# Two-layer block kernel: decay rows, mask and splits of the gated delta inverse moved, weight splits ahead of columns and taps

## What is computed

```
for l in range(2):                                        # first block
    mod = (silu(c) @ ada_w[l] + ada_b[l])                 # shift, scale, gate of three sublayers
    x = x + 0.5 * gate0 * swiglu(adaln(x), ffn1_w13[l], ffn1_w2[l])
    p = adaln(x) @ w_in[l] + b_in[l]
    y = concat([rms(nsa(p)), rms(short_conv(p)), gated_deltanet(p), mlstm(p)])
    x = x + gate1 * (y @ w_out[l])
    x = x + 0.5 * gate2 * swiglu(adaln(x), ffn2_w13[l], ffn2_w2[l])
for l in range(2):                                        # second block
    x = x + concat([sgu(n), diff_attention(n)]) @ w_out2[l]
    up = rms(x) @ w_up[l]; a, b = split(causal_conv3(up)) # 2 x 2816 channels
    x = x + (silu(a) * b) @ w_down[l]
return rms(x)
```

## Time and profile before

| What | Value |
|---|---|
| median of 3 runs | 3474.03 us (3472.71 to 3477.58) |
| the profiled execution's own time | 3467.37 us |
| its span | 3465.6 us |
| mean granted TensorE clock | 0.995 |
| PE busy | 3361.1 us, 97% |
| DVE busy | 2305.6 us, 67% |
| ACT busy | 1327.3 us, 38% |
| POOL busy | 459.7 us, 13% |

### The profile page before, as it was taken

One profiled execution on the slowest core, in us unless ns is written; L12 is line 12 of the kernel. 1 busy time (PEld: TensorE's weight loads), 2 busy tenths in 40 slices (PEclk: granted clock), 3 DMA queues, 4 the chain that ended last, 5 costly groups with the idle time before them and its releaser, 6 DMA issues.

```text
span 3465.6 us, 51220 instructions
## 1 busy us (share of the span) xinstructions
PE 3361.1 (97%) x19868; PEld 2826.2 (82%) x19868; DVE 2305.6 (67%) x3623; ACT 1327.3 (38%) x2102; POOL 459.7 (13%) x341
## 2 busy tenths in 40 slices
PE   7999999999999999999999999999999999999999
PEld 5989877788888898987778888887788888778887
DVE  6878757667776677785766877657666525766642
ACT  5324344525333432434452533343443324443321
POOL 2000200142000400020014200021200011120002
PEclk9999999999999999999999999999999999999999
DMA  6463522103443345442210344321223322123332
GB/s 256 142 216 134 165 80 86 42 20 122 162 161 99 103 155 204 140 158 86 85 37 26 121 171 146 103 84 55 80 91 97 106 97 73 56 79 97 97 105 83
DMA packets 88631, 383.02 MB, mean 111 GB/s; under 512 B 9774, under 2 KB 10926, under 8 KB 77704
## 3 DMA queue, kind: packets, MB, share of 16 engines
q1 hardware_dynamic: 88456, 380.62, 33.2%
HBM read 378.46 MB, written 2.12 MB: 110 GB/s over the span
## 4 chain that ended last, share of the span: by engine, by line
PE 83%; DVE 9%; ACT 3%; DMA 3%; issue 2%; POOL 0%; SPq 0%; ACTq 0%; DVEq 0%; POOLq 0%
PE bank L3415 6%; PE bank L3416 6%; PE bank L3417 6%; PE bank L3504 4%; PE bank L3505 4%; PE bank L3506 4%; PE bank L3661 4%; PE bank L3458 4%; PE bank L3459 4%; PE bank L3460 4%; PE bank L3663 4%; PE bank L3662 4%; PE bank L3531 3%; PE bank L3532 3%; PE bank L3533 3%; DMA adaw<-in_ada_w 2%
## 5 line engine op out<-in xcount | busy, mean ns | idle before, releaser
L1975 DVE TENSOR_TENSOR wL<-wR,wH 128x1024 fp32r<-128x1024 f32 (+2 forms) x160 | 209.7, 1310 | 207.9 <-ACT wH L1274 207.8
L1274 ACT ACTIVATE wH<-wR 128x1024 fp32r<-128x1024 f32 (+2 forms) x158 | 174.8, 1107 | 373.6 <-PE bank L3417 303.8
L3661 PE MATMUL bank<-hH,wH 128*128 128x512 f32 x672 | 283.6, 422 | 0.0
L3663 PE MATMUL bank<-hL,wH 128*128 128x512 f32 x672 | 264.5, 394 | 0.0
L3662 PE MATMUL bank<-hH,wL 128*128 128x512 f32 x672 | 263.5, 392 | 0.0
L3531 PE MATMUL bank<-gHc,wH 128*128 128x512 f32 x660 | 256.9, 389 | 0.0
L3532 PE MATMUL bank<-gHc,wL 128*128 128x512 f32 x660 | 256.9, 389 | 0.0
L3533 PE MATMUL bank<-gLc,wH 128*128 128x512 f32 x660 | 256.8, 389 | 0.0
L3415 PE MATMUL bank<-hH,wH 128*128 128x512 f32 x640 | 249.9, 391 | 4.1 <-DVE wL L1975 4.1
L3504 PE MATMUL bank<-hH,wH 128*128 128x512 f32 x640 | 249.8, 390 | 1.2 <-DVE wL L2031 1.2
L3416 PE MATMUL bank<-hH,wL 128*128 128x512 f32 x640 | 249.6, 390 | 0.0
(11 more groups left out here) (533 smaller groups left out, 8762.1 us busy)
## 6 DMA issues: line engine op xcount, KB each, us to landing
RW<-in_ffn_wq SPq DMA_DIRECT2D x80, 1024.0 KB, 5.7
adaw<-in_ada_w SPq DMA_DIRECT2D x144, 512.0 KB, 4.4
wR<-in_w_up SPq DMA_DIRECT2D x88, 512.0 KB, 3.6
wR<-in_ffn_w SPq DMA_DIRECT2D x56, 704.0 KB, 4.1
wR<-in_w_mix SPq DMA_DIRECT2D x76, 512.0 KB, 3.6
wR<-in_w_down SPq DMA_DIRECT2D x32, 704.0 KB, 4.0
wR<-in_w_in SPq DMA_DIRECT2D x40, 512.0 KB, 3.6
wR<-in_ffn_w SPq DMA_DIRECT2D x16, 512.0 KB, 3.6
```

What stands on the lines that cost most here:

```text
L3661: pe.matmul(o, wH[n][:, k, :], hH[:, k, :], start=k == 0, stop=False)
L3663: mm = pe.matmul(o, wH[n][:, k, :], hL[:, k, :], start=False, stop=k == KT - 1)
```

## The change

In the first block's delta mixer: the beta rows come ahead of K's turn on TensorE; the decay rows (now banks 4 and 5, `decay_rows`) move into the last level, in place of fillers; EGP's exponentials move behind the levels on ACT; the reduction L2622 moves behind the copies of K and the products KBT on DVE. The last level takes N itself in place of POOL's masked copy, so POOL masks five levels (the semaphore counts follow: c_nk 20, and EGP behind the others on c_a). The splits `early_low` move: two after the second head of the last level, two before each copy of U; `lo_third` moves behind the copies. ACT's halves stay where they are. One of the six inputs' high parts gets another place (PS is still needed then). In `ffn` the column of turn 6 moves behind `group2`, `group1` and `single` of turn 7, and that of turn 7 behind `group3`. In `up2`, in turn 1 only, ACT's and DVE's split of the sixth unit move ahead, to before the silu and before the taps of the second half. In the first layer TensorE gets 24 fillers ahead of its wait for the modulation.

```diff
@@ -129,7 +129,7 @@
 Y_EARLY = (PA_Q, PA_Q + 1, PB_B, PB_B + 1, PD_O, PD_O + 1)
-Y_HIGH = (PA_VSW, PS, PB_X, PB_X + 1, PC_V, PC_V + 1)
+Y_HIGH = (PA_VSW, PB_C, PB_X, PB_X + 1, PC_V, PC_V + 1)
 NE = len(Y_EARLY)
@@ -1697,6 +1694,9 @@
         for p in range(2):
+            act.wait_ge(S.c_gp, at(S.c_gp, p + 1))
+            act.activation(EGP[p][:, :], bank[4 + p][:, :], ACT.Exp).then_inc(S.c_a, 1)
+        for p in range(2):
             act.wait_ge(S.c_w, at(S.c_w, p + 1))
@@ -1908,11 +1908,14 @@
             last_tap(i, 0, b)
+            first = isinstance(i, int) and i == 1
+            if first:
+                hi_ahead(ubase, i, 1, tiles)
             act.wait_ge(S.f_conv, at(S.f_conv, 4 * i + 2))
             act.activation(sil[:, :], xn[:, 0, :], ACT.Silu).then_inc(S.sil, 1)
             act.wait_ge(S.w_used, at(S.w_used, ubase + 2 * i + 2))
             last_tap(i, 1, b + 1)
-            if later(i):
+            if later(i) and not first:
                 hi_ahead(ubase, i, 1, tiles)
@@ -2165,14 +2168,15 @@
                 single(f, Q_A, "1b", 2, 2)
-                columns((ADA_DN1, ADA_DN2)[f] + m)
+                columns((ADA_DN1, ADA_DN2)[f] + m - 1)
             dve.wait_ge(S.w_used, at(S.w_used, udn + m + 1))
             add_to_x(m, 2 + m % 2, sub, S.x_mid)
             if m + 2 < KT:
                 down_low(udn, m + 2, 0)
-            if m < KT - 1:
+            if m < KT - 2:
                 columns((ADA_DN1, ADA_DN2)[f] + m)
         group3(f, Q_A)
+        columns((ADA_DN1, ADA_DN2)[f] + KT - 1)
         u = udn + KT
@@ -2618,8 +2622,6 @@
             norm_out(n)
-        dve.wait_ge(S.o_sq, at(S.o_sq, 2))
-        dve.tensor_reduce(HR[:, 0, :], YQ[:, :, :], AX.X, ALU.add).then_inc(S.o_v, 1)
@@ -2632,6 +2634,8 @@
             dve.tensor_tensor(KBT[p][:, :], pm[:, PC_K + p, :], bank[4 + p][:, :], ALU.mult).then_inc(S.c_v1, 1)
+        dve.wait_ge(S.o_sq, at(S.o_sq, 2))
+        dve.tensor_reduce(HR[:, 0, :], YQ[:, :, :], AX.X, ALU.add).then_inc(S.o_v, 1)
         dve.wait_ge(S.sm_v, at(S.sm_v, n_bg(1)))
@@ -2693,6 +2697,12 @@
+        def early_low(i0):
+            for n in range(2):
+                i = i0 + n
+                dve.wait_ge(S.y_hi, at(S.y_hi, (3, 5, 1)[i0 // 2] + n))
+                dve.tensor_tensor(YL[i][:, :], pm[:, Y_EARLY[i], :], YH[i][:, :].bitcast(F32), ALU.subtract).then_inc(S.y_lo, 1)
         def level(k, last=False):
@@ -2703,13 +2713,10 @@
                     dve.tensor_scalar(PP[h][r, :, c], v4(6 + h % 2)[r, :, c], -1.0, None, ALU.mult).then_inc(S.c_pu, 1)
+                    if h == 1:
+                        early_low(4)
                 else:
                     dve.tensor_tensor(PP[h][:, :, :], PP[h][:, :, :], v4(6 + h % 2), ALU.subtract).then_inc(S.c_pu, 1)
-        def early_low(i0):
-            for n in range(2):
-                i = i0 + n
-                dve.wait_ge(S.y_hi, at(S.y_hi, (3, 5, 1)[i0 // 2] + n))
-                dve.tensor_tensor(YL[i][:, :], pm[:, Y_EARLY[i], :], YH[i][:, :].bitcast(F32), ALU.subtract).then_inc(S.y_lo, 1)
         for k in range(1, 7):
@@ -2724,17 +2731,11 @@
                     dve.scalar_tensor_tensor(y, y, col(C_MIXB + j), bank[5][:, :], ALU.mult, ALU.mult).then_inc(S.n_out, 1)
-            elif k == 2:
-                early_low(4)
-            elif k == 3:
-                early_low(0)
-            elif k == 4:
-                early_low(2)
-            elif k == 5:
-                lo_third(U_OUT + 2, NE)
         for p in range(2):
+            early_low(2 * p)
             dve.wait_ge(S.c_u, at(S.c_u, p + 1))
             dve.tensor_copy(UU[p][:, :, :], v4(p)).then_inc(S.c_uc, 1)
+        lo_third(U_OUT + 2, NE)
@@ -3124,12 +3125,15 @@
             taps(i, 0, b)
+            first = isinstance(i, int) and i == 1
+            if first:
+                lo(ubase + 2 * i + 3, tiles, 1)
             taps(i, 1, b + 1)
             if not later(i):
                 lo(ubase + 4, tiles, 0)
             dve.wait_ge(S.sil, at(S.sil, i + 1))
             dve.tensor_tensor(gf[:, :], xn[:, 1, :], sil[:, :], ALU.mult).then_inc(S.g_mul, 1)
-            if later(i):
+            if later(i) and not first:
                 lo(ubase + 2 * i + 3, tiles, 1)
@@ -3245,9 +3249,9 @@
         pool.wait_ge(S.c_a, at(S.c_a, n_c_seg(TT * H)))
-        for k in range(1, 7):
+        for k in range(1, 6):
             level(k)
-        pool.wait_ge(S.c_nk, at(S.c_nk, 24))
+        pool.wait_ge(S.c_nk, at(S.c_nk, 20))
         for h in range(H):
@@ -3896,9 +3900,6 @@
             turn_tiles(2 + p, lambda t: pm[:, PC_V + p, t * P:(t + 1) * P], S.c_vt)
-        pe.wait_ge(S.n_out, at(S.n_out, 6))
-        for p in range(2):
-            turn_tiles(p, lambda t: pm[:, PC_K + p, t * P:(t + 1) * P], S.c_kt)
         pe.wait_ge(S.a_yv, at(S.a_yv, n_a_y(TT - 1)))
@@ -3907,20 +3908,16 @@
             mm.then_inc(S.c_bp, 1)
-        pe.wait_ge(S.n_out, at(S.n_out, 8))
+        pe.wait_ge(S.n_out, at(S.n_out, 6))
         for p in range(2):
-            r = R_AL + 2 * p
-            for e in range(2):
-                mm = pe.matmul(bank[6 + p][half(e), :], bc(ident[:, r + e:r + e + 1], [P, HD]), pm[:, PS, :],
-                               start=True, stop=True)
-            mm.then_inc(S.c_gp, 1)
+            turn_tiles(p, lambda t: pm[:, PC_K + p, t * P:(t + 1) * P], S.c_kt)
         pe.wait_ge(S.c_v1, at(S.c_v1, n_c_ktc(2)))
         pe.wait_ge(S.c_a, at(S.c_a, n_c_vtc(2)))
         for h in range(H):
             pe.matmul(bank[h][:, :], bc(ident[:, R_AL + h:R_AL + h + 1], [P, P]), pm[:, PS, :], start=True,
                       stop=True).then_inc(S.c_grp, 1)
         pe.wait_ge(S.c_v1, at(S.c_v1, n_c_kbt(2)))
-        pe.wait_ge(S.c_a, at(S.c_a, n_c_egp(2)))
+        pe.wait_ge(S.n_out, at(S.n_out, 8))
@@ -3984,10 +3981,19 @@
+        def decay_rows(p):
+            r = R_AL + 2 * p
+            for e in range(2):
+                mm = pe.matmul(bank[4 + p][half(e), :], bc(ident[:, r + e:r + e + 1], [P, HD]), pm[:, PS, :],
+                               start=True, stop=True)
+            mm.then_inc(S.c_gp, 1)
         def level(k, last=False):
             for h in range(H):
-                pe.wait_ge(S.c_nk, at(S.c_nk, 4 * k + h - 3))
+                if not last:
+                    pe.wait_ge(S.c_nk, at(S.c_nk, 4 * k + h - 3))
                 if k == 1:
@@ -3996,7 +4002,7 @@
                     if last:
-                        mm = pe.matmul(bank[h][half(1), block64(t, 0)], NK[h % 2][half(0), t, half(1)],
+                        mm = pe.matmul(bank[h][half(1), block64(t, 0)], NN[h][half(0), t, half(1)],
                                        XX[h][half(0), t, half(0)], start=True, stop=True)
@@ -4004,14 +4010,14 @@
                 if last and h == 3:
-                    warm(1, 4)
+                    decay_rows(0)
                 if h:
                     square(k, h - 1, last)
                 if last and 0 < h < 3:
-                    warm(h, 3)
+                    warm(1, 3)
+            if last:
+                decay_rows(1)
             square(k, H - 1, last)
-            if last:
-                warm(1, 4)
         level(1)
@@ -4128,6 +4134,7 @@
         if l == 0:
+            warm(24)
             pe.wait_ge(S.mod_set, at(S.mod_set, 2))
```

More of the change, by code:

```diff
@@ L338 @@
     "o_rs": 3, "o_t": 6, "c_kt": 2, "c_v1": 16, "c_vt": 2, "c_a": 24, "c_bp": 2, "c_gp": 2, "c_grp": 4,
-    "c_v2": 20, "c_kk": 4, "c_kq": 4, "c_qd": 3, "c_xt": 4, "c_nk": 24, "c_z": 24, "c_zc": 24, "c_xz": 20,
+    "c_v2": 20, "c_kk": 4, "c_kq": 4, "c_qd": 3, "c_xt": 4, "c_nk": 20, "c_z": 24, "c_zc": 24, "c_xz": 20,
     "c_xu": 20, "c_zp": 24, "c_pu": 24, "c_u": 2, "c_uc": 2, "c_w": 2, "c_wc": 2, "c_wp": 3, "c_vn": 8,
@@ L477, in n_c_vtc, with n_c_seg, n_c_x0 @@
     return k
+def n_c_seg(k):
+    return 2 + k
+def n_c_x0(k):
+    return 18 + k
 def n_c_egp(k):
[L481 to L489, removed]
+    return 22 + k
 def n_a_hc(k):
@@ L1654, in mix_c @@
                                    ACT.Copy).then_inc(S.c_a, 1)
-                for p in range(2):
-                    act.wait_ge(S.c_gp, at(S.c_gp, p + 1))
-                    act.activation(EGP[p][:, :], bank[6 + p][:, :], ACT.Exp).then_inc(S.c_a, 1)
                 for h in range(H):
```

## The result

Timed beside the kernel before in the same rounds, the changed kernel took 3448.7 us (median of 4 runs, 3445.7 to 3452.0) against 3474.5: a ratio of 0.9922, 95% interval 0.9909 to 0.9934, 25.8 us less at the medians. Run once more later it was 3450.3 against 3475.6, 0.9933 (0.9919 to 0.9947). The forecast was 3451.8. The profiled execution of after took 3445.7 us, its span is 3443.9, which is 21.7 us shorter than the span of before.

The account below looks back on a forecast made before the run. TensorE, busy for 97% of the span, was taken as the bound, with gains only in its waits and half clock. 6.5 + 4.1 + 3.4 + 7.6 + 0.6 = 22.2 us off 3474.0 gave 3451.8, range 3443 to 3464.

Parts of the forecast that it names:

- The bound: Whole kernel: TensorE, busy for 97% of the span, so time is gained only where it waits or runs at half clock.
- Boundaries, -6.5: Swiglu chunk boundaries: splits ahead of the column remove four TensorE waits for L2031, -7.0 us, less small charges: -6.5.
- The give-back of 0.5: Raw-weight requests waiting behind column 7 in each layer's first sublayer: 0.25 us charged twice against the boundaries' gain.
- `up2`, -4.1: Sixth unit's split in `up2` moves ahead of the second taps, so TensorE's two waits for L1975 go: -4.1 us.
- Clock, -3.4: Two short half-clock drops, after the third boundary and the second `up2` wait, vanish with those waits: -3.4 us.
- Inverse, levels 3 to 5, -4.6: Without splits on DVE, TensorE paces these levels at 6.1 us each instead of 22.9 together: 4.6 us less per layer.
- Last level, +1.1: Last level of the inverse: decay rows come in, masks and some fillers go; net +1.1 us per layer.
- Ahead of the inverse, -0.3: Mixer before the inverse: DVE's work unchanged in sum, only its small waits go: -0.3 us per layer.
- Behind it, 0: Scan to output projection: splits and POOL's product slow each other, second copy of U just within 1.1 us slack: 0.
- Start, -0.6: First layer's wait for the modulation: 24 fillers raise the clock, limited by the third unit's split: -0.6 us.
- the mixer: Both layers' delta mixers: -4.6 + 1.1 - 0.3 = -3.8 us per layer, -7.6 in all.
- the partial case: Rival, 3458 us, chance 0.20: POOL paces the levels at 6.6 us and splits collide with it at the scan.

Follow-up runs that it names:

- the two halves of the edit: Kernel before with only the mixer's output splits moved: 0.9968; kernel before with the mixer's other edits and the splits left in the levels: 1.0021.
- the rest alone: Kernel before with the mixer's edits (unmasked last level, decay rows, exponentials, beta rows, reduction) but splits left in the levels: 1.0021, once more 1.0015.
- the fillers brought POOL's masks onto DVE's products: Kernel after with five TensorE fillers in its wait for N ahead of the second pair's products (L3926): ratio to before 0.9931.

## Why the prediction was right, step by step

**The bound.** Right: TensorE sets the time, and every wait that was named went. The gains below are the shifts of the same matmul between the traces of before and after, taken on both sides of each place.

**Boundaries, -6.5.** Measured -8.1 (2.0 each: the wait of 1.8 and the restart behind it, 0.38 us for the first matmul where it is 0.28 without the wait; the prediction left the restart out). The give-back of 0.5 didn't come, and neither did column 7: it waits for its weights as before, and the first sum came 1.7 us earlier, forecast 1.8.

**`up2`, -4.1.** Measured -4.7 in after and alone, no wait of the product's behind it; here too the restart was left out.

**Clock, -3.4.** This step failed in the profiled execution: the two drops went and gave 3.1 us, but the double one at 1557.5 came and took 3.3, so the total outside the start and the mixer's edits is the same, four stretches of 3.4 us in each. That before's profile had no such stretch there was chance. As a mean over the profiles the step holds at the places that it names. In seven profiles with the boundary waits 8 of 28 boundaries had a drop, in seven without them none of 28; with the `up2` waits 9 of 14, without them none of 14. That is 1.1 + 1.3 drops an execution, at 1.7 us each 4.1 us. Left out was also that two of before's four short drops follow another wait and stay. And left out was what the change does to the clock itself: the decay rows taken from between K's turning and the heads' rows open the wait for N to 2.47 us.

**Inverse, levels 3 to 5, -4.6.** Measured -5.0: 6.10, 6.05 and 5.82 us. That DVE had bounded them is shown by the two halves of the edit, and that TensorE is next by its 0.23 us of idle time in a level. POOL's bound of 5.85 us was too high, because that time was itself slowed by the splits; alone the masks take 4.99.

**Last level, +1.1.** Measured 8.31 us, +1.1, with the rest alone too.

**Ahead of the inverse, -0.3.** Wrong in size and in place. At full clock the first level starts 0.5 us earlier; in after it starts 0.2 later because of the half clock, yet level 2 starts 0.9 earlier, since level 1 is bounded by DVE and a late TensorE keeps POOL's masks off one of its products. Level 1 was not looked at in the prediction.

**Behind it, 0.** Right: slack of 1.1 us, 0.7 used. Which pair would be slowed was wrong: the second, not the first. The first pair slowed the product's first half to 2.61 us, and that moved its second half onto the second pair; that POOL could pay was left out.

**Start, -0.6.** Measured +0.1 to +0.2. The split of the third unit doesn't move, and an earlier first product only waits for it. With the mean squares at half clock the fillers even end after modA.

**Sum.** 8.1 + 4.7 + 9.3 (4.8 and 4.5, the mixer's two layers) - 0.2, with 3.1 - 3.3 for the clock, are the 21.7 us of the profiles. The forecast, 22.2, had the mixer 1.7, the boundaries 1.6 and `up2` 0.6 too small, the clock 3.6 and the start 0.8 too large: the errors cancel, and that the sum came so close is luck. The medians fell by 25.8 and 25.3 us, 3 more than forecast; they also hold how many stretches at half clock came in their executions, which one profile of each kernel can't show. Of the rivals, the partial case fell at both points: levels at 6.0 and not 6.6, and a collision that stays within the slack.

## What to carry to other kernels

Work that only has to be done by a certain stage belongs behind the stage where its engine is the bound: six splits moved from DVE's full levels to its idle time in the last level and ahead of the copies of U gave 5 us a layer by themselves. Before work is taken out of a gap between two waits of TensorE, add up the idle time that it leaves in one piece. And a speed-up of an engine that releases another moves the other's work too: the fillers brought POOL's masks onto DVE's products and gained nothing. Last, where the clock drops by chance, a difference of a few us is told by the starts of the same work in two traces, and not by two medians.

## What was not expected of the hardware

The granted clock fell to 0.50 at the wait for N of 2.5 us in all 12 layers of the six profiles that have it, and in none of the 14 layers in which that wait is 0.8 or 1.8 us, nor in the two where fillers fill it. Waits of 2.2 us for PTR, which are in every kernel, were followed by a drop in 27 cases of 28. Waits of 1.5 to 2.7 us at the boundaries were followed by one in 8 cases of 28, and not in the longest (2.7 us, in the rest alone), those of 2.1 in `up2` in 9 of 14, and some stretches in which TensorE was busy throughout ran at half clock as well (1557.47 to 1564.30). So a drop is not explained by the length of the wait ahead of it alone, and executions of one kernel differ by 13 to 17 us (before, the rest alone).

DVE and POOL slowed each other, not DVE alone: four masks took 5.85 us beside the splits and 4.99 without, the two halves of POOL's product 3.84 beside them and 2.49 without, and which of the two engines paid differed between two pairs of splits of the same shape.
